# A transformer layer with 32 routed experts on one Trainium2 core: expert rows summed by TensorE instead of scattered and gathered

## What is computed

```
x += W_o( sig(g_a) * W_A(MLA(h)) + sig(g_b) * W_B(GLA(h)) )      h = RMSNorm(x)
x += HierMoE(RMSNorm(x));  y = RMSNorm(x)

HierMoE: every token takes the best of 4 groups, in it the best 2 of 8 experts,
         gates = softmax(two logits) * group probability
expert e: (silu(xb @ w_gate[e]) * (xb @ w_up[e])) @ w_down[e]     w_gate, w_up 1024x512, w_down 512x1024
y = segment_sum(out * gate, token)                                 each token is the sum of its two experts' rows
```

## Time and profile before

| | |
|---|---|
| median of 3 runs | 1119.4 us (1118.56 to 1120.49) |
| the profiled execution | 1122.52 us, span 1120.7 us |
| mean granted TensorE clock | 0.962 of full |
| TensorE (PE) busy | 1025.1 us, 91% |
| weight loads (PEld) | 701.9 us, 63% |
| VectorE (DVE) / ScalarE (ACT) / GpSimd (POOL) busy | 380.1 / 281.6 / 223.6 us |
| DMA | 267.57 MB, 239 GB/s over the span |

### The profile page before, as it was taken

How to read it: one execution, slowest core, us unless ns; L and a number is a source line. 1 busy time by engine, 2 the same in 40 slices (tenths; PEclk the granted TensorE clock), 3 DMA queues, 4 the chain that set the end, 5 groups by cost and what they waited for, 6 DMA issues and landing times.

```text
span 1120.7 us, 15303 instructions
## 1 busy us (share of the span) xinstructions
PE 1025.1 (91%) x6339; PEld 701.9 (63%) x6339; DVE 380.1 (34%) x727; ACT 281.6 (25%) x454; POOL 223.6 (20%) x129
## 2 busy tenths in 40 slices
PE   8999999999999999999999899977888889877886
PEld 6996777779999879999998333333333333333332
DVE  7246332233587491421344322111011111111117
ACT  5435434346446442222213100000000000000003
POOL 0331112112312256434330011110011110110000
PEclk9999999999999989999999999999888999998898
DMA  9332411212211213253285999999999999999993
GB/s 225 81 88 79 164 50 39 57 39 74 60 48 39 67 57 91 80 164 100 80 351 224 346 427 426 426 425 427 427 427 427 427 428 427 428 427 425 426 410 136
DMA packets 108943, 267.57 MB, mean 239 GB/s; under 512 B 21821, under 2 KB 88797, under 8 KB 95666
## 3 DMA queue, kind: packets, MB, share of 16 engines
q1 hardware_dynamic: 104178, 258.06, 60.0%
q0 software_dynamic: 4704, 8.64, 2.0%
HBM read 256.12 MB, written 18.17 MB: 245 GB/s over the span
## 4 chain that ended last, share of the span: by engine, by line
PE 37%; DMA 24%; DVE 4%; issue 2%; ACT 2%; POOL 1%; SPq 0%; DVEq 0%; ACTq 0%; POOLq 0%
DMA we<-in_w_exp_up 24%; PE proj L1051 16%; PE proj L1533 12%; PE proj L1549 3%; DVE ors L2089 1%; PE bank L1425 1%; DVE xsT L2536 1%; PE bank L1559 1%; PE proj L1331 0%; ACT ex L1873 0%; PE proj L1535 0%; DVE gqk L2361 0%; POOL wlo L905 0%; PE bank L1027 0%; PE bank L1626 0%
## 5 line engine op out<-in xcount | busy, mean ns | idle before, releaser
L1533 PE MATMUL proj<-we,xsT 128*64 128x512 f32 x512 | 252.1, 650 | 66.4 <-DMA we<-in_w_exp_up 58.6
L1535 PE MATMUL proj<-we,xsT 128*64 128x512 f32 x512 | 252.5, 651 | 0.0
L905 POOL TENSOR_TENSOR wlo<-raw,whi 128x1024 fp32r<-128x1024 f32 x68 | 155.7, 2290 | 397.9 <-PE proj L1051 373.4
L1533 PEld LDWEIGHTS proj<-we,xsT 128*64 128x64 f32 x512 | 73.6, 150 | 212.2 <-issue 198.1
L1051 PE MATMUL proj<-hT_hi,whi 128*128 128x272 f32 x688 | 147.7, 296 | 2.0 <-DVEq L2313 2.0
L1051 PE MATMUL proj<-hT_hi,wlo 128*128 128x272 f32 x688 | 145.3, 293 | 0.0
L1051 PE MATMUL proj<-hT_lo,whi 128*128 128x272 f32 x688 | 145.3, 293 | 0.0
L2528 DVE TENSOR_TENSOR hg<-hg,proj 64x512 f32<-64x512 f32 x32 | 22.1, 690 | 310.2 <-ACT hg L2043 293.9
L2043 ACT ACTIVATE hg<-proj 64x512 f32<-64x512 f32 x30 | 17.7, 590 | 422.0 <-PE proj L1535 422.0
L1549 PE MATMUL proj<-we,hT 128*64 128x512 f32 x256 | 115.2, 593 | 1.1 <-DVE hT L2531 1.1
L1550 PE MATMUL proj<-we,hT 128*64 128x512 f32 x256 | 115.2, 592 | 0.0
(11 more groups left out here) (364 smaller groups left out, 1430.9 us busy)
## 6 DMA issues: line engine op xcount, KB each, us to landing
we<-in_w_exp_gate SPq DMA_DIRECT2D x31, 2048.0 KB, 32.0
we<-in_w_exp_up SPq DMA_DIRECT2D x31, 2048.0 KB, 36.6
we<-in_w_exp_down SPq DMA_DIRECT2D x31, 2048.0 KB, 39.0
raw<-in_w_in SPq DMA_DIRECT2D x43, 512.0 KB, 3.8
x_rows<-in_x_prompt SPq DMA_DIRECT2D x8, 512.0 KB, 5.2
raw<-in_w_branch_b SPq DMA_DIRECT2D x8, 512.0 KB, 3.9
raw<-in_w_out SPq DMA_DIRECT2D x8, 512.0 KB, 4.0
zc<-expert_out SPq DMA_DIRECT2D x4, 1024.0 KB, 16.7
```

What stands on the lines that cost most here:

```text
L905: nc.gpsimd.tensor_tensor(lo[:, 0:c], raw[n % NRAW][:, 0:c], hi[:, 0:c].bitcast(F32), ALU.subtract).then_inc(w_split, 1)
L1533: pe.matmul(proj[0:SLOTS, s, 0, :], xsT[:, k, cols], wg[:, k * FF:(k + 1) * FF], start=(k == 0), stop=(k == KD - 1))
L1535: mm = pe.matmul(proj[64:64 + SLOTS, s, 0, :], xsT[:, k, cols], wu[:, k * FF:(k + 1) * FF], start=(k == 0), stop=(k == KD - 1))
```

## The change

1. **No scatter, no read back.** `expert_out`, its clearing, the 30 scatters, the five reads and `add_gated`, `second_rows` are gone. Gates are no longer applied at the end: a table `slot_gates` (slot, expert) is made with `on_lanes` and multiplied in with the silu product (`gated`).
2. **Picks instead.** After a down, ScalarE writes the result rounded to fp32r into `yo_hi` (two copies of 64 rows by 512), VectorE the rest into `yo_lo`; both experts of a pair lie one above the other in 128 lanes. VectorE makes `pair_pick` (128 slots by 544 tokens, ones and zeros). In the next pair, TensorE multiplies for each of the five token tiles the picks with high and low halves (`tile_rows`: four fp32r products of 512 columns), before steps k = 3, 5, 7 of up(1) and k = 0, 2 of the down(0) that follows. VectorE adds each tile into `x_rows` (`add_tile`). All five go through the same two banks, so each waits for the add before it, and `turn_rows` waits for the last. Pairs 1 to 14 have this (14 times); the first pair has none yet, and the last pair's rows are picked among the last two experts' work (`rows_ahead`).
3. **Last experts.** `turn_hidden` of expert 30 moves inside the up of expert 31 (before k = 4), `rows_ahead(0)` before the last step of expert 30's up.
4. **Values' turn first.** `chunk_scores(0)` moves behind `turn_values(6)`; ScalarE loads its exponential table early, by a one-element instruction.
5. **Low halves.** GpSimd makes three of the five (`EARLY_LOW`), one after the other, VectorE the last two; ScalarE makes the last two high halves before it turns to the gate of `ga` 5.

```
-            if first_pair(it, m):
-                pe.wait_ge(picks_ready, 1)
+            def in_up(k):
+                if k in UP_PICKS:
+                    pair_rows(it, m, UP_PICKS.index(k))
+            def in_down(k):
+                if k in DOWN_PICKS:
+                    pair_rows(it, m, len(UP_PICKS) + DOWN_PICKS.index(k))
...
-                up(s, slice(s * SLOTS, (s + 1) * SLOTS), w[0], w[1], up_done)
-                if u or not first_pair(it, m):
-                    go_down(it, u - 1)
+                up(s, slice(s * SLOTS, (s + 1) * SLOTS), w[0], w[1], up_done, in_up if s and beside else None)
+                if u or beside:
+                    go_down(it, u - 1, in_down if s and beside else None)
                 if s:
+                    if beside:
+                        pe.wait_ge(rows_added, it * (NT * NSETS) + NT * m)
                     turn_rows(it * (16 * NSETS) + 16 * m + 32)
...
+        def tile_rows(i, lanes_, done, at=0):
+            r = ROWS[i]
+            for half in range(2):
+                pe.matmul(bank[0:r, at + half, :], pair_pick[lanes_, i * P:i * P + r], yo_hi[lanes_, half, :], start=True, stop=False)
+                mm = pe.matmul(bank[0:r, at + half, :], pair_pick[lanes_, i * P:i * P + r], yo_lo[lanes_, half, :],
+                               start=False, stop=True)
+            mm.then_inc(done, 1)
+        def pair_rows(it, m, i):
+            if i:
+                pe.wait_ge(rows_added, it * (NT * NSETS) + NT * (m - 1) + i)
+            else:
+                pe.wait_ge(yo_ready, it * (2 * NSETS) + 2 * m)
+            tile_rows(i, slice(0, P), rows_picked)
...
         def up_half(k):
+            if k == KD // 2:
+                pe.wait_ge(act_done[0], PAIRS)
+                turn_hidden(0, hT2_done)
...
-        up(0, slice(0, SLOTS), w0[0], w0[1], up_done)
-        pe.wait_ge(act_done[0], PAIRS)
-        turn_hidden(0, hT2_done)
+        up(0, slice(0, SLOTS), w0[0], w0[1], up_done, first_tile)
         up(1, slice(SLOTS, P), w1[0], w1[1], up_done, up_half)
...
-        for i in range(2, 4):
-            last_rows(0, i, True, False)
-            second_rows(i, False)
+        for i in range(2, 4):
+            rows_ahead(i)
+            last_rows(0, i, False, False)
             last_rows(1, i, False, True)
...
                 pe.wait_ge(vtok_ready, 5)
                 decays(1)
-                pe.wait_ge(vtok_ready, 6)
-                chunk_scores(0)
                 pe.wait_ge(bS_ready, 2)
...
             turn_values(j - 1)
+            if j == 7:
+                pe.wait_ge(vtok_ready, 6)
+                chunk_scores(0)
```

```
 ScalarE
+                nc.scalar.activation(st_x[:, 1, 0:1], eps_col[:, :], ACT.Exp)
...
-        gate_value(0, "ga", 5)
         o_high(3)
         o_high(GH)
+        gate_value(0, "ga", 5)
...
+                if u or not first_pair(it, m):
+                    rows_high(it, u - 1)
 VectorE
+        dve.wait_ge(ob_ready, EARLY_LOW)
+        for h in range(EARLY_LOW, GH + 1):
+            dve.wait_ge(ob_high, h + 1)
+            part = output_part(h)
+            v.tensor_tensor(ob_lo[part], gqk[part], ob_hi[part].bitcast(F32), ALU.subtract).then_inc(ob_ready, 1)
...
+                if s and beside:
+                    for i in range(len(UP_PICKS) + 1):
+                        pair_rows(it, m, i)
                 dve.wait_ge(silu_done, it * (2 * NSETS) + u + 1)
-                gated(s, act_done[s])
-                if u or not first_pair(it, m):
-                    rows_out(it, u - 1)
+                gated(s, it * (2 * NSETS) + u, act_done[s])
                 if s:
+                    if beside:
+                        for i in range(len(UP_PICKS) + 1, NT):
+                            pair_rows(it, m, i)
                     dve.wait_ge(xsT_done, it * NSETS + m + 2)
                     turned_rows(xsT_copied)
...
-                dve.wait_ge(hT2_done, it * (2 * NSETS) + u + 1)
-                hidden_copy(s, hT2_copied[s])
+                    dve.wait_ge(hT2_done, it * (2 * NSETS) + u + 1)
+                    hidden_copy(s, hT2_copied[s])
+                    make_picks(it * NSETS + m)
+                    rows_low(it, u - 1)
+                else:
+                    if beside:
+                        rows_low(it, u - 1)
+                    dve.wait_ge(hT2_done, it * (2 * NSETS) + u + 1)
+                    hidden_copy(s, hT2_copied[s])
```

More of the change, by code:

```diff
@@ L115, in shape_constants @@
     put("token", r[:, None] + P * np.arange(NT) - float(VACANT))
-    put("half", 1.0 * (r[:, None] >= SLOTS))
     return c
 EARLY_GR = 4
+EARLY_LOW = 3
 EARLY_CUM = 4
@@ L1518, in _ @@
         pe.wait_ge(last_gates_ready, 1)
[L1519 to L1524, removed]
+        on_lanes(bank[:, 3, 0:NBLK], 0, token_at, True, False)
+        on_lanes(bank[:, 3, 0:NBLK], 1, token_at, False, True).then_inc(second_done, 1)
         def turned(rows_):
@@ L1530, in up @@
             for k in range(KD):
-                if half and k in (0, KD // 2):
+                if half:
                     half(k)
@@ L1546, in down @@
             for k in range(4):
-                if half and k in (0, 2):
+                if half:
                     half(k)
@@ L1607, in _ @@
                     down(0, we[SPARE][2], more_down)
+                    pe.wait_ge(more_yo, b + 1)
+                    for i in range(NT):
+                        if 0 < i < NT - 1:
+                            pe.wait_ge(more_added, b * NT + i)
+                        tile_rows(i, slice(0, SLOTS), more_picked, 2 if i == NT - 1 else 0)
+                    pe.wait_ge(more_added, b * NT + NT)
                     for k in range(KD):
@@ L2505, in _ @@
         run(v.tensor_tensor(gate[:, 1, :], gate[:, 0, :], rd, ALU.mult))
-        run(v.tensor_tensor(both_gates, O[:, :, :, NE - 2:NE], gate[:, :, :].unsqueeze(3).to_broadcast([P, 2, NT, 2]), ALU.mult))
-        v.tensor_tensor(last_gates[:, :, :], both_gates[:, 0], both_gates[:, 1], ALU.add).then_inc(last_gates_ready, 1)
+        for c in range(2):
+            last = v.tensor_tensor(token_at[:, c], is_blk[:, c], across(gate, c, NBLK), ALU.mult)
+        last.then_inc(last_gates_ready, 1)
+        for s in range(2):
+            lane = slice(s * SLOTS, (s + 1) * SLOTS)
+            step(v.tensor_copy(pair_tokens[lane, :], G1[lane, 0:NE].rearrange("p (q s) -> p q s", s=2)[:, :, s]))
         run(v.tensor_tensor(nbe, starts[0:1, 1:NE + 1].unsqueeze(1).to_broadcast([1, NOVER, NE]),
@@ L2572, in _ @@
         with dve.If(n_more > 0):
[L2573 to L2574 removed]
+            for i in range(NT):
+                pair_rows(ROUNDS, 0, i)
             dve.wait_ge(xs_loaded, 16 * PAIRS)
```

217 lines of the change are left out of this document (101 added, 116 removed).

## The result

| | before | changed kernel |
|---|---|---|
| median | 1119.95 us (4 runs) | 1133.81 us (4 runs, 1129.98 to 1134.19) |
| ratio of the changed kernel to before | | 1.0113, 95% interval 1.0096 to 1.0131 |
| profiled span | 1120.7 us | 1131.8 us |
| mean granted clock | 0.962 | 0.989 |

The account below looks back on a forecast made before the run. The weight stream bounds the pairs; the change makes TensorE their limit. Terms on the 1119.4 us base: -1.7 - 1.4 + 9.7 - 0.3 (expert 30's weight wait) - 2.2 - 3.1 = +1.0, so 1120.4 us, range 1110 to 1127.5.

Parts of the forecast that it names:

- the last experts: From expert 30's up to the end of down(31): 24.5 us instead of 26.7, so -2.2 us.
- the output: From the end of down(31) to VectorE's last operation: 18.3 us instead of 21.4, so -3.1 us.
- Low halves: At `wb` 0, TensorE's 1.4 us wait for GpSimd's last low halves goes: -1.4 us, bounds 0 and 1.4.
- The pair: In the 14 pairs with picks, TensorE needs 30.4 us a pair instead of 29.71: +9.7 us in all.
- The seams: In the pairs, entering and leaving each full-height pick block between 64-column halves costs TensorE 0.34 us.
- the stall: In each pair, TensorE stands 0.4 us before the fourth token tile, waiting for the add before it.
- the product: In the pick blocks, an fp32r product of 512 columns takes 0.215 us, 0.86 us a block; upper bound 0.236.
- The first pair: The pair ahead of the 14 with picks: no change, 0 us.
- The base: Whole kernel: the profiled execution, 1122.5 us in all, lies 3.1 us above the median of 1119.4.
- the values' turn: At the first chunk's scores, values' turn and early exponential table save 1.7 us of the `vtok` wait, bounds 0 and 2.7.
- A: Rival, pairs: cheaper blocks; a 29.7 us pair gives 1110.6 us, at 29.0 or less weights bind, floor 1100.6; chance 0.24.
- B: Rival, pairs: the picks' chain to `yo_lo` is late, TensorE stands 0.5 us a pair; 30.9 us, 1127.4 us; chance 0.16.

Follow-up runs that it names:

- e1: Changed kernel with ScalarE's gate of ga 5 again ahead of the last two high halves; 1128.37 us.
- e9: e1 with the low halves made as in the kernel before, all five on GpSimd (two, one, two); 1128.46 us.
- e5: Kernel before with only the values' turn ahead of the first chunk's scores and the early exponential table load; 1117.95 us, ratio 0.9975 to before.
- e4: Changed kernel with the same pick products in three blocks instead of five, odd tiles in two other banks; 1118.28 us, ratio 0.9962 to before.
- e3: Changed kernel with five tiny unread full-height products (16 columns) more in each of 14 pairs; 1166.62 us.
- e8: Changed kernel with one more unread filling product ahead of the gate tables in the routing; 1132.63 us.
- e2: Changed kernel without the pick products and adds inside the pairs, still without scatters; 1105.33 us.
- e6: Changed kernel with the edits of e4 and e1 together; 1112.34 us, ratio 0.9934 to before.
- e7: e6 with the next pair's row turn moved inside down, into the block of tile 4; 1105.10 us, ratio 0.9868 to before.
- e10: e7 with the low halves made as in the kernel before, all five on GpSimd; 1103.66 us, ratio 0.9847 to before.
- e11: e7 run again unchanged, on the same chip as e10; 1106.04 us, ratio 0.9872 to before.

## Why the prediction was wrong

Right were the mechanism (TensorE becomes the limit of the pairs, no wait for weights), the sign there, and the terms for the last experts and the output. These steps failed:

1. **Low halves: forecast -1.4, in truth +2.3 us up to 430 us.** The step costed GpSimd and VectorE and left out the third thing that this edit moves: ScalarE's gate of `ga` 5 goes behind two high halves, one of which needs `gqk` from VectorE (3.2 us at least, by the table above). And even without that, GpSimd's three subtractions in a row delay `wlo` (e1: 1.8 us, gone in e9), so the 1.4 us of the `ob_lo` wait, which did go, are paid back. The 2.3 us are read against before's profile, itself 2.7 us slow behind 411 us; against e5, which has the old low halves and gate, it is 4.9 us.
2. **The pair: 30.4 forecast, 30.78 measured, 14 x 0.38 = +5.3 us.** The seams were right (0.35 for 0.34, e4), so was the stall (the step into the fourth block is 0.37 us longer than into the others, for 0.40). Mis-sized was the product: 0.23 us instead of 0.215, nearly the upper bound of 0.236 from the 272-column ones. Twenty products make 0.3 us of the 0.38. The prediction had both bounds and the time for the dear one (1126.3), and took the cheap one on the thought that a fixed surplus doesn't grow with length; it does grow. It also said that the trace of before has no such product. The trace has five, in the GLA's gate logits (both operands fp32r in the kernel, 96 rows instead of 128, 512 columns), four of them where the clock falls and one at full clock:

```profile
258.71 0.40 PE L1234 MATMUL bank<-w_g,glr 96*32 96x512 f32 x1
258.94 0.41 PE L1051 MATMUL proj<-hT_hi,whi 128*128 128x272 f32 x2
```

The next product starts 0.23 us after it. That row would have settled the term before any run.
3. **The first pair: 0 forecast, +1.9 measured.** A stretch at half clock. In the profiles of e3, e4, e5 and e8 it is there too (23.8 to 24.0 us, clock 0.93), in those of before, e1, e2, e6 and e9 it isn't (22.1 to 22.3, clock 1.00). In e7, e10 and e11 it is there as well (clock 0.92, and 0.51 from 621.97 to 625.40 us in e7); their first pair reads 22.1 to 22.3 only because its second landmark, the next turn, stands two steps of down, 1.7 us, earlier. e5 is the old kernel but for one edit at 300 us. What decides it is open. It isn't the gap in the routing (e8), and nothing shows that this change brings it.
4. **The base.** The profiled execution of before was taken to be 3.1 us above a median of 1119.4, and the same offset was put on the changed kernel. But 42 later runs of before, in three groups, had medians of 1119.9 to 1121.2, and the changed kernel's profiled 1133.6 is within 0.3 us of its median. A median of three runs was trusted to more than its 2 us of spread, and part of the profiled execution's extra time can be seen: 2.7 us at half clock behind 411 us, which e5, with the same code there, has not.

The four make 3.7 + 5.3 + 1.9 + 3.1 = 14.0 us of the 13.4 missed; against that, TensorE's lead over before was 1.2 us already at 22 us (a matter of the execution: the first `hT_hi` products start at 16.3 to 17.6 us in the profiles, 17.2 in before's), and 0.6 us were lost between 430 us and the first `turn_rows`: 13.4.

What held: the values' turn (-1.7 forecast, 1.7 in e5); last experts, from expert 30's up at 1086.37 to the end of down(31) at 1111.08, 24.7 us for 24.5; output, from there to the end of VectorE's last operation, 18.3 for 18.3:

```profile
1086.37 0.59 PE L1505 MATMUL proj<-we,xsT 128*64 128x512 f32 x1
...
1111.08 0.50 PE L1664 MATMUL proj<-yo_hi,pair_pick 128*128 128x512 f32 x1
...
1126.89 2.47 DVE L2696 SCALAR_TENSOR_TENSOR zc<-x_rows,st_x,g_fin 128x1024 f32<-128x1024 f32 x2
```

Of the rivals, A (the weights bind) happened only once the blocks were grouped and the turn had moved into one (e7). Its first case doesn't add up: half of the 0.34 us and no stall would be 30.4 - 0.85 - 0.4 = 29.15 us a pair, not 29.7. B gave the right side and nearly the pair (30.9), but not by its mechanism: TensorE's products never waited for `yo_lo` (its weight loads, which run ahead, did, 0.8 us a pair, and the first block is no longer than the second), the products were dearer and an early queue was reordered.

## What to carry to other kernels

When a stage is bound by a transfer, the other engine's spare time is a budget: compare the whole price of what is put there, seams included, with it. Here the five blocks cost 6.7 us a pair. The old pair's length left 5.65, and the stream without scatters, once it binds, only 28.77 - 24.06 = 4.7. The same products in three blocks, with the following turn in the last one, fitted. For each moved instruction, write down what now stands behind it on its own engine; a gate that the diff moved by two lines cost over 3 us. Look through the whole trace for the operation that you are about to price, in stages that the change doesn't touch too. A time that agrees with a theory doesn't confirm it (e1, e8); the waits do.

## What the runs showed of the hardware that was not expected

- A full-height fp32r product of 512 columns steps by 0.23 us inside a block, 0.45 ns a column, and 0.33 to 0.34 as the first of one. The 272-column ones come every 0.1255 us, 0.46 ns a column: hardly cheaper by length.
- A DMA share of 0.99 to 1.01 is there with TensorE starving (before) and with no wait for weights at all (changed kernel, e4). The time from issue to landing and the waits tell the cases apart, the share doesn't.
- Two of VectorE's `gqk` products (L2361 of before, L2400 of the changed kernel) took 1.42 us at 400.75 us of before with GpSimd idle, 3.99 at 405.47 beside GpSimd's subtraction of a weight tile, and 5.22 us at 411.98 of the changed kernel beside the three low halves in a row. How long these took went with what GpSimd did. The Trainium skill says in "GPSIMD Engine Reference", Specifications, that GpSimd shares its SBUF interfaces with VectorE and contends with VectorE instructions that have two SBUF inputs; these rows agree, though no run here tested it by itself.
